# A two-layer decoder trunk on one core: the first weight split, and where the state stage puts its small products

## The reference, cut to what matters

```
x: (256, 2048)
layer 0:  h = rms_norm(x);  z = gelu(h @ gm_w_in);  u, v = split(z);  v = layer_norm(v)
          x += (u * (causal(w_s) per head @ v + b)) @ gm_w_out
layer 1:  h = rms_norm(x);  u = h @ s5_w_in
          s_t = lam_bar * s_(t-1) + b_bar u_t      (128 groups x 64 complex states)
          y = Re(C s) + D u;  val, gate = split(gelu(y) @ s5_w_out);  x += val * sigmoid(gate)
both:     x += (silu(h @ w1) * (h @ w3)) @ w2                       (h = rms_norm(x))
          x += sigmoid(rms_norm(x) @ w_gate) * (p @ w_proj)
out = rms_norm(x)
```

## Time and profile before

| | us |
|---|---|
| median of three runs (2258.19, 2258.64, 2260.22) | 2258.64 |
| the profiled execution | 2255.93 |
| its span, first to last instruction | 2254.0 |
| PE busy in the span | 2238.2 (99%) |
| DVE busy | 1440.8 (64%) |
| ACT busy | 1022.7 (45%) |

### The profile page before, as it was taken

One profiled execution on the slowest core, in us unless ns is written; L12 is line 12 of the kernel. 1 busy time (PEld: TensorE's weight loads), 2 busy tenths in 40 slices (PEclk: granted clock), 3 DMA queues, 4 the chain that ended last, 5 costly groups with the idle time before them and its releaser, 6 DMA issues.

```text
span 2254.0 us, 28581 instructions
## 1 busy us (share of the span) xinstructions
PE 2238.2 (99%) x11378; PEld 1843.4 (82%) x11378; DVE 1440.8 (64%) x1579; ACT 1022.7 (45%) x1241; POOL 495.5 (22%) x469
## 2 busy tenths in 40 slices
PE   9999999999999999999999999999999999999998
PEld 7888888888888888888878888888888888888886
DVE  7878767667766766666667866555555445555665
ACT  5544454444444444445444354444444344444444
POOL 1245325455665544301002100000000000000001
PEclk9999999999999999999999999999999999999999
DMA  8667788888887888887789867677766667767764
GB/s 289 194 198 231 228 243 266 241 249 254 251 243 221 255 263 240 247 260 266 236 244 331 309 207 231 201 217 222 215 214 209 194 194 221 220 213 230 228 214 141
DMA packets 347838, 525.81 MB, mean 233 GB/s; under 512 B 105929, under 2 KB 125273, under 8 KB 347193
## 3 DMA queue, kind: packets, MB, share of 16 engines
q1 hardware_dynamic: 336784, 488.50, 71.1%
q0 software_dynamic: 8320, 30.75, 3.7%
q10 hardware_dynamic: 2600, 4.74, 0.6%
HBM read 473.05 MB, written 50.86 MB: 232 GB/s over the span
## 4 chain that ended last, share of the span: by engine, by line
PE 94%; DVE 3%; DMA 3%; issue 0%; ACT 0%; SPq 0%; ACTq 0%; DVEq 0%
PE PS L1553 60%; PE PS L1559 30%; DVE WLO L1059 1%; PE PS L1764 1%; DMA HT<-zd 1%; DMA ROOTU<-rootd 1%; DMA RAW<-in_ple_w_gate 1%; PE PS L1673 0%; PE PS L1584 0%; DMA X<-in_x 0%; PE PS L1789 0%; DMA rootd<-ROOT 0%; PE PS L1781 0%; DVE Z L1340 0%; PE PS L1842 0%
## 5 line engine op out<-in xcount | busy, mean ns | idle before, releaser
L1553 PE MATMUL PS<-WHI,OP 128*128 128x512 f32 x6208 | 1540.7, 390 | 0.1
L1059 DVE TENSOR_TENSOR WLO<-RAW,WHI 128x1024 fp32r<-128x1024 f32 x783 | 1027.9, 1324 | 655.8 <-ACT WHI L767 652.3
L1553 PEld LDWEIGHTS PS<-WHI,OP 128*128 128x128 f32 x6208 | 1160.8, 188 | 245.4 <-issue 4.6
L767 ACT ACTIVATE WHI<-RAW 128x1024 fp32r<-128x1024 f32 x783 | 825.5, 1061 | 939.6 <-PE PS L1559 811.1
L1559 PE MATMUL PS<-WLO,OP 128*128 128x512 f32 x3104 | 830.4, 389 | 2.1 <-DVE WLO L1059 1.9
L1559 PEld LDWEIGHTS PS<-WLO,OP 128*128 128x128 f32 x3104 | 582.2, 188 | 125.1 <-DVE WLO L1059 4.1
L751 POOL TENSOR_TENSOR ON<-X,GF 128x1024 f32<-128x1024 f32 x3 | 9.9, 3297 | 945.1 <-DVE X L1395 945.1
L654 POOL TENSOR_TENSOR TA<-BRAW,FAC 128x64 f32<-128x64 f32 x16 | 9.8, 613 | 317.2 <-DMA BRAW<-in_s_b_im 317.2
L1071 DVE TENSOR_TENSOR OP<-HT,OP 128x512 fp32r<-128x512 f32 x50 | 34.6, 733 | 55.3 <-ACT OP L782 55.3
L782 ACT ACTIVATE OP<-HT 128x512 fp32r<-128x512 f32 x50 | 28.9, 625 | 74.5 <-DMA HT<-zd 74.5
L815 ACT ACTIVATE S<-PS,RC 128x512 f32<-128x512 f32 x66 | 41.7, 683 | 30.7 <-PE PS L1559 30.7
(11 more groups left out here) (213 smaller groups left out, 959.9 us busy)
## 6 DMA issues: line engine op xcount, KB each, us to landing
RAW<-in_ffn_w SPq DMA_DIRECT2D x528, 512.0 KB, 4.6
RAW<-in_gm_w_in SPq DMA_DIRECT2D x64, 512.0 KB, 4.9
RAW<-in_ple_w_gate SPq DMA_DIRECT2D x64, 512.0 KB, 4.9
RAW<-in_s_w_out SPq DMA_DIRECT2D x64, 512.0 KB, 5.1
zd<-ZT SPq DMA_DIRECT2D x37, 512.0 KB, 3.7
HT<-zd SPq DMA_DIRECT2D x148, 128.0 KB, 5.7
RAW<-in_gm_w_out SPq DMA_DIRECT2D x32, 512.0 KB, 4.9
RAW<-in_s_w_in SPq DMA_DIRECT2D x32, 512.0 KB, 5.6
```

What stands on the lines that cost most here:

```text
L767: A_.activation(hi_of(t), RAW[:, t % RING, :], ACT.Copy).then_inc(hi_ready, 1)
L1059: V_.tensor_tensor(lo_of(t), RAW[:, t % RING, :], hi_of(t).bitcast(F32), ALU.subtract).then_inc(lo_ready, 1)
L1553: T_.matmul(dst[:, th, :], x_part, WHI[:, slot, f], start=first and kk == 0 and part == 0, stop=False)
```

## The change

At the start ACT rounds the first weight tile ahead of the first quad of x instead of behind it, and PE turns the quads 1, 2, 3 behind the tiles 0, 1, 2 instead of one at once and the others behind the tiles 0 and 2. In the state stage `into_states` of both duos of a column stands behind the same tile (the scan of the second stays one tile later on DVE, where it was), and six of the eight `out_of_states` stay while those of duos 1 and 3 move by two tiles, behind the tiles at which the next column's `into_states` stand. `OUT_AT` was W0 + 20, 22, 28, 30, 36, 38, 44, 46 and is W0 + 20, 24, 28, 32, 36, 38, 44, 46; `INTO_AT` was W0 + 16, 17, 24, 25, 32, 33, 40, 41 and is W0 + 16, 16, 24, 24, 32, 32, 40, 40. (Duo 5's place, W0+38, is the same in both.)

```diff
-INTO_AT = [W0 + 8 * (d // 2) + 16 + d % 2 for d in range(DUOS)]
-OUT_AT = [W0 + 8 * (d // 2) + 20 + 2 * (d % 2) for d in range(DUOS - 2)] + [W0 + 44, W0 + 46]
+INTO_AT = [W0 + 8 * (d // 2) + 16 for d in range(DUOS)]
+OUT_AT = [W0 + 4 * d + 20 for d in range(DUOS - 3)] + [W0 + 38, W0 + 44, W0 + 46]
...
             act.wait_ge(vec_ready, 1)
+            section()
             high(0)
-            section()
             section()
             high(1)
...
-                    if W0 + g == INTO_AT[d] + 1:
+                    if W0 + g == INTO_AT[d] + 1 + d % 2:
                         scan(d)
...
             turn(0)
-            turn(1)
 
             def prologue(t):
-                if t in (0, 2):
-                    turn({0: 2, 2: 3}[t])
+                if t < 3:
+                    turn(t + 1)
```

## The result

The changed kernel took 2267.23 us in the median of six runs (2265.09 to 2270.05), the kernel before 2258.91 beside it (2257.80 to 2260.22). The ratio is 1.0039, interval 1.0030 to 1.0049: slower by 8.3 us, outside the range of the prediction and on the side that it gave 0.08.

What follows compares the result with a forecast made beforehand. PE was taken as the bound, busy 2238.2 of 2254.0 us. Start +1.1, weight stream +0.3 and state stage -1.8 gave -0.4, so 2258.64 became 2258.2 us; range 2255.2 to 2261.5.

Steps and rivals of the forecast that it cites:

- -1.8 for the stage: State stage: fewer changes of work on PE, 1.4 us for four pairs and 0.4 behind W0+24 and W0+32; between -1.0 and -2.1.
- The start's +1.1: Start: tile 0 later +0.5 us, a turn added between tiles +0.9, a wait for x's quad 2 gone -0.3.
- rival 2: Start: the clock falls before tile 0 while PE is idle, 0 to 3.6 us more, half is +1.8, 2260.0; chance 0.12.
- The weight stream: Behind the start, tile 8 as tightest: its weight load may land later; bounded by 0 and 1.5 us, taken as 0.3.
- The borders in the stage: State stage: PE's changes of work, 0.17 us each; 0.34 saved per pair, 0.2 more behind W0+24 and W0+32.
- The margin of W0+29: State stage, tile W0+29: its `WLO` is done by 19.3, PE comes at 21.2; margin 1.9 us against 1.6 before.
- rival 4: State stage, W0+29 and W0+37: a scan's length lands on PE, 3.6 us at each, +7.2, 2265.4; chance 0.06.
- What would show it wrong: First tile before 9.4; tile 0 matmuls at twice 227 ns pitch; PE wait near 33 us or behind W0+28 or W0+37.
- rivals 2 and 3: Start: clock falls before tile 0 (2260.0, chance 0.12); weight stream starves tiles 8 to 10 (1.5 us, 2259.4, chance 0.09).

Runs made afterwards that it cites:

- warm_start: The start's edits alone plus 18 identity transposes on PE between quad 0's transposes and tile 0, against the kernel before: 2258.20 us, ratio 1.0011.
- into_only: Only `INTO_AT` and the scan's place changed, `OUT_AT` and start as in the kernel before: 2255.54 us, ratio 0.9993.
- phase64: Both state tables changed, start as in the kernel before, plus 64 small transposes on PE near 562 us, long ahead of the stage: 2263.45 us, ratio 1.0033.
- state_only: The state stage's tables alone changed, start as in the kernel before: 2260.49 us, ratio 1.0018.
- root_late: Kernel before, but DVE waits for `win`'s transposed roots at W0+9 instead of W0+7 and ACT takes the first `Z` one tile later: 2252.82 us, ratio 0.9984.
- state_store: State tables alone changed, plus ACT's store of the turned `u` one tile earlier, ahead of `y_high` of duo 3, against the kernel before: 2259.99 us, ratio 1.0019.
- start_only: The start's edits alone (first weight tile ahead of quad 0, late turns), state tables as in the kernel before: 2260.85 us, ratio 1.0019.
- turn_only: Only the late turns of quads 1, 2, 3; ACT does quad 0 first as in the kernel before: 2259.76 us, ratio 1.0014.
- out_only: Only `OUT_AT` changed (`out_of_states` of duos 1 and 3 moved to W0+24 and W0+32), rest as in the kernel before: 2256.83 us, ratio 1.0004.

## Why the prediction was wrong

The forecast was 2258.2, made of +1.1 and +0.3 for the start and -1.8 for the stage. Point by point:

**The start's +1.1 was right and not all.** Tile 0 at 9.84 against 9.9, the first `WHI` at 7.02 against 6.9, and the turn between tiles at 0.90 came as forecast; `warm_start` shows +0.9 at tile 3. The first step that failed is that the sum puts the clock at nothing and leaves it to rival 2, with a chance of 0.12. I had the gap ahead of tile 0 at 2.8 us, and held against a fall that nothing before shows one and that PE starts again before 10 us; but before had no such gap in so light a stretch, so its silence was no evidence. The gap was 2.24 and the clock fell, in all four kernels that turned late with nothing in the gap. The Trainium skill, "TensorE: Matmul & The Clock Gate", HAM oscillation, spoke for this rival, and the trace bears it out, with a wait shorter than those of the page's example. By the tile's rows it cost 2.91 + 1.88 instead of 2.08 + 1.07 in modelled lengths; from tile 0's start to tile 1's 5.22 us passed where 3.62 was reckoned, so +1.6, near the +1.8 that the rival priced.

**The weight stream starved tile 6, not tile 8.** This is the second step that failed. I bound this term by 0 and 1.5 and looked only at the tile with the least margin. But the edit moves DVE's work for quad 1 ahead of tile 2's `WLO`, and so tile 6's load by 3.9 us. A load that had been well before GpSimd's broadcasts came to stand beside them, and took 12.7 us instead of 5.2. A margin in the trace of before says nothing where the order behind it changes: every load that waits for a moved step had to be followed, not the tightest one. And the case was not independent of rival 2: without the 1.6 us of the clock tile 6 doesn't wait at all, as `warm_start` shows, and the term is what I reckoned, 0.5 us at tile 8 where I took 0.3.

**The borders in the stage were right.** Counted were 0.34 a pair and 0.54 where `out_of_states` stands ahead of it; the starts of the `WLO` matmuls give 0.34 to 0.35 (after, `into_only`) and 0.52 to 0.56 (after, `phase64`). Where no gap of the other kind covers them, that makes the -1.8.

**Two terms of the stage were missing.** This is the third step that failed: both were put at nothing. First the supply of instructions: 2.3 us inside the group (from one record's start to the next), and 1.7 for the clock behind it. I reckoned the merged group as its parts less their borders. Nothing in the trace of before has such a run, and I should have bounded the unseen thing from above. Second ACT's chain. The margin of W0+29 was worked out for DVE and PE and held; rival 4 did not come to pass. For ACT I wrote that it stands in `y_high` and that the weight tile it rounds next is ready long before, and left out that `store_u` and `spread_u` are queued behind it and `take_y` behind them: in after 0.9 us up to the end of W0+40, in `phase64` 1.7. The sum of the stage becomes -1.8 + 2.3 + 1.7 + 0.9 = +3.1. The trace of after has +3.1 from W0+12 to the last tile of the stage, and the median of `state_only` is +4.2 with an interval from +2.0 to +6.1.

**A reading that was wrong.** The prediction says that no wait of the earlier trace rows lies in the state stage. The larger one, 1.63 us, lies in W0+10. It is no part of the change's loss by itself, but it was the one place in the stage where waiting less did pay, as `root_late` shows.

**What would show it wrong** was named aright: matmuls of tile 0 at twice their pitch (those behind 10.85 us), and a wait of PE near 33 us. The chances were not: 0.87 for no change took rivals 2 and 3 for nearly independent, though the one brings on the other, and had no price for the supply of instructions or for ACT's chain.

**What stays open.** I moved the instruction stream by one distance only, so I don't know which groups meet a gap and which don't; the 0.43 us in `state_store`, whose stream on PE is that of `state_only`, which has no gap there, says that it isn't decided by place alone. Of the start's +4.5 in the median I can't give the parts: the traces give 1.6 for the clock at tile 0 and 1.9 for tile 6, plus the second fall of the clock where it comes, and each is one execution. The roots' 4.3 us between the two profiles I call scatter; that the change has no part in them is argued from the other traces, and not tested.

## What to carry to other kernels

A step that is moved later can cost a gap twice: once as a wait, and again as a tile at half the clock, so before work is taken out of a short gap of TensorE ask what keeps the engine at work through it. Follow every engine's queue behind the moved step to the transfers that it releases, and look what they will stand beside. And where runs of the same kernel scatter, look whether a wait on a round trip through memory differs between their traces: here, moving that wait behind two tiles gave more here than all the borders together.

## What the runs showed of the hardware

- A gap of 2.2 to 2.5 us of TensorE behind the light work of the start brought the granted clock from 1.00 to 0.50 in all four kernels that had it. Waits amid full tiles did so in some traces (2.01 us at tile 6 in `start_only`, 1.88 in `turn_only`) and not in others (1.87 at tile 6 in after).
- Not every kind of work holds the clock: behind 64 transposes of 32x32 in a row (4.38 us, no idle time) the next 8 matmuls took 3.42 us instead of 2.1. The 224 small records of the state stage's group, 6.0 us in `phase64`, did hold it (2.11 us behind them).
- A long run of short instructions can outrun their supply: a group of 448 instructions of TensorE that lasts 6.0 us by itself stopped for 2.1 to 2.6 us with all operands there, and not at all once the stream ahead was 128 instructions longer. Gaps of 0.4 to 0.6 us came in runs of 256 and 320 instructions too (`state_store`, `out_only`). Each ended 1.3 to 1.5 us behind a 16 KB transfer of instructions.
- A 512 KB load took 12.7 us from issue to landing when it was issued beside two broadcasts of 1 MB, 8.1 us at the same place with the broadcasts moved away, and 5.2 us when issued 3.9 us earlier.
